# A four-layer hybrid decoder step: at three layer ends GpSimd adds the squares of the residual, and TensorE sums them with one product

## The reference

```python
def rms_norm(x, g):
    xf = x.astype(F32)
    y = xf * lax.rsqrt(jnp.mean(xf * xf, axis=-1, keepdims=True) + EPS)
    return (y * g.astype(F32)).astype(x.dtype)
...
for layer in range(DEPTH):
    h = rms_norm(x, g[0])
    y, ... = mixer(h, ...)
    x = x + rms_norm(y, g[1])
    h = rms_norm(x, g[2])
    y = memory_cross_attn(h, mem_k[layer], mem_v[layer], ...)
    x = x + rms_norm(y, g[3])
```

## Time and profile before

| | us |
|---|---|
| median of 3 runs | 2000.47 (1999.58 to 2001.61) |
| the profiled execution: its time | 2002.32 |
| the profiled execution: span from first to last instruction | 2000.5 |

### The profile page before, as it was taken

One profiled execution on the slowest core, in us unless ns is written; L12 is line 12 of the kernel. 1 busy time (PEld: TensorE's weight loads), 2 busy tenths in 40 slices (PEclk: granted clock), 3 DMA queues, 4 the chain that ended last, 5 costly groups with the idle time before them and its releaser, 6 DMA issues.

```text
span 2000.5 us, 35695 instructions
## 1 busy us (share of the span) xinstructions
PE 1946.4 (97%) x13930; PEld 1763.9 (88%) x13930; DVE 1243.0 (62%) x2220; ACT 929.5 (46%) x1555; POOL 1011.8 (51%) x1251
## 2 busy tenths in 40 slices
PE   9999999999999999999999999999999999999997
PEld 7998988798888998797889999998997889999976
DVE  6887434346887778655147877777464157874452
ACT  4767422344655555342354444443243347774333
POOL 5767623126555655150356666665641347776602
PEclk9999999999999999999999999999999999999998
DMA  5444567435444444486353444444586344455860
GB/s 172 141 137 143 160 220 261 167 100 175 130 131 133 139 135 153 124 298 235 116 169 109 131 131 131 144 144 149 161 306 221 130 146 137 139 158 167 286 231 27
DMA packets 332615, 324.64 MB, mean 162 GB/s; under 512 B 19768, under 2 KB 313056, under 8 KB 332448
## 3 DMA queue, kind: packets, MB, share of 16 engines
q1 hardware_dynamic: 330944, 321.49, 50.4%
q10 hardware_dynamic: 1504, 0.87, 0.2%
HBM read 292.16 MB, written 29.61 MB: 161 GB/s over the span
## 4 chain that ended last, share of the span: by engine, by line
PE 61%; DVE 9%; ACT 3%; issue 1%; DMA 1%; POOL 1%; SPq 0%; ACTq 0%; DVEq 0%
PE ps L773 8%; PE ps L774 8%; PE ps L778 8%; PE ps L1460 4%; PE ps L1263 3%; PE ps L1469 2%; PE ps L1526 2%; PE ps L763 2%; DVE work L2550 2%; PE ps L764 2%; PE ps L765 2%; PE ps L890 1%; PE ps L1337 1%; PE ps L1604 1%; PE ps L1543 1%
## 5 line engine op out<-in xcount | busy, mean ns | idle before, releaser
L1695 POOL TENSOR_TENSOR wl<-raw,wh 128x256 fp32r<-128x256 f32 x1216 | 1004.3, 861 | 956.6 <-ACT wh L1720 956.3
L1720 ACT ACTIVATE wh<-raw 128x1024 fp32r<-128x1024 f32 x302 | 309.8, 1053 | 207.9 <-PE ps L778 51.6
L773 PE MATMUL ps<-Hh,wh 128*128 128x320 f32 x1200 | 369.3, 321 | 2.5 <-DVE gate_area L2570 0.9
L774 PE MATMUL ps<-Hl,wh 128*128 128x320 f32 x1200 | 357.3, 311 | 0.0
L773 PEld LDWEIGHTS ps<-Hh,wh 128*128 128x128 f32 x1200 | 227.8, 190 | 10.3 <-DVE gate_area L2570 1.7
L774 PEld LDWEIGHTS ps<-Hl,wh 128*128 128x128 f32 x1200 | 227.9, 190 | 2.2
L2265 DVE TENSOR_SCALAR work<-ps 128x512 f32<-128x512 f32 (+8 forms) x220 | 100.4, 474 | 169.3 <-PE ps L873 39.8
L778 PE MATMUL ps<-Hh,wl 128*128 128x320 f32 x1200 | 200.7, 309 | 0.0
L778 PEld LDWEIGHTS ps<-Hh,wl 128*128 128x128 f32 x1200 | 182.6, 188 | 0.1
L773 PE MATMUL ps<-Oh,wh 128*128 128x320 f32 x512 | 152.2, 310 | 3.7 <-DVE Ol L3011 3.7
L774 PE MATMUL ps<-Ol,wh 128*128 128x320 f32 x512 | 151.1, 308 | 0.0
(11 more groups left out here) (442 smaller groups left out, 3923.6 us busy)
## 6 DMA issues: line engine op xcount, KB each, us to landing
raw<-rg_w_in SPq DMA_DIRECT2D x128, 256.0 KB, 3.6
raw<-hg_w_in SPq DMA_DIRECT2D x128, 256.0 KB, 5.0
raw<-ssd_w_in SPq DMA_DIRECT2D x96, 256.0 KB, 4.1
work<-cache_mem_k SPq DMA_DIRECT2D x40, 512.0 KB, 6.7
work<-cache_mem_v SPq DMA_DIRECT2D x40, 512.0 KB, 5.2
raw<-rg_w_out SPq DMA_DIRECT2D x64, 256.0 KB, 3.6
raw<-x_w_k SPq DMA_DIRECT2D x64, 256.0 KB, 3.6
raw<-x_w_v SPq DMA_DIRECT2D x64, 256.0 KB, 3.8
```

What stands on the lines that cost most here:

```text
L773: pe.matmul(ps[:, bank, 0:n], high(half, k), mh[:, k, 0:n], start=(k == 0), stop=False)
L774: pe.matmul(ps[:, bank, 0:n], high(half, k), ml[:, k, 0:n], start=False, stop=False)
L1695: ins = pool.tensor_tensor(out, src, wh[:, parted(n) % HALVES, r:r + 2].bitcast(F32), ALU.subtract)
L1720: act.activation(wh[:, nx.n % HALVES], raw[:, slot, :, half * P:(half + 1) * P], ACT.Copy).then_inc(hi_ready, 1)
```

## The change

`SQ[:, 0]` becomes the sum of all eight tiles by seven additions on POOL, each of which waits for its square and for POOL's own addition before. POOL counts `sq_pooled` after the last one. PE waits for that count and makes one product with ones where it made eight. `sq_pooled` is counted on the semaphore `consts`, behind the two counts that this has from the start of the kernel, so the instruction lists show a wait for `consts`.

```diff
+        shared = {"sq_pooled": ("consts", 1, 2), "lam_abs": ("par_read", 1, 2), ...
...
+        POOLED = KD - 1
...
+            def sum_pooled(L, n, bank):
+
+                pe.wait_ge(*past("sq_pooled", L + 1))
+                pe.matmul(ps[:, bank, 0:NT], ones[:], SQ[:, 0], start=True, stop=True).then_inc(S("ssq_full"), 1)
...
                 values(5, 0)
                 values(5, 1)
-                sum_squares(5 + 4 * L, 7)
+                sum_pooled(L, 5 + 4 * L, 7)
                 pe.wait_ge(*past("at_v_ready", XH * (L + 1) + 2))
                 values(4, 0)
                 values(4, 1)
...
+            def add_squares(L):
+                n = 5 + 4 * L
+                for k in range(1, POOLED + 1):
+                    pool.wait_ge(*past("sq_ready", n * KD + k + 1))
+                    if k > 1:
+                        steps.sync()
+                    ins = pool.tensor_tensor(SQ[:, 0], SQ[:, 0], SQ[:, k], ALU.add)
+                    if k < POOLED:
+                        steps.did(ins)
+                    else:
+                        ins.then_inc(S("sq_pooled"), 1)
+
             for n in PARTED:
+                if n in MIX_AT[1:]:
+                    add_squares(MIX_AT.index(n) - 1)
                 low(n)
```

More of the change, by code:

```diff
@@ L133, in trunk @@
         sems = {}
-        shared = {"lam_abs": ("par_read", 1, 2), "lb_diff": ("par_read", 1, 3), "sd_sel": ("par_read", 1, 4),
+        shared = {"sq_pooled": ("consts", 1, 2), "lam_abs": ("par_read", 1, 2), "lb_diff": ("par_read", 1, 3), "sd_sel": ("par_read", 1, 4),
                   "sd_dt_abs": ("par_read", 1, 5), "sd_dta": ("par_read", 1, 6),
```

## The result

The changed kernel is slower: 2006.3 us in the median of 7 runs, against 2000.59 us of 7 runs of the kernel before, a ratio of 1.0031 with a 95% interval of 1.0019 to 1.0042. I had forecast 1999.9 us and no measurable change, with a range to 2005.5. Measured three times more, each time beside the kernel before, it gave 1.0025 (1.0012 to 1.0038), 1.0028 (1.0017 to 1.0040) and 1.0023 (1.0014 to 1.0032). The loss is small, some 3 to 6 us, but it is there every time.

The account below looks back on a forecast made before the run. PE, busy 97% of the span, pays the eight products in full; removing 14 instructions an end, less POOL's late sum and half clock, wins 0.2 us, three ends 0.6: 2000.47 - 0.6 = 1999.9 us, range 1992.5 to 2005.5.

Parts of the forecast that it names:

- The port: Layer ends: DVE's residual and POOL's additions take turns on SBUF, 1.51 us a tile; PE waits 2.8 us for the sum.
- The addition: POOL at layer ends: additions of 128x320 spaced 0.84 us, some 0.95 us each with a hand-over as they depend on each other.
- The logarithm: ACT at a layer end: its logarithm begins at 1622.3 against 1623.10, 0.8 us won.
- The clock at the ends: Behind PE's 2.8 us wait: half clock at most of the three ends, leaving 0 to 0.3 us won, 0.2 taken.
- three ends 0.6: Whole kernel: 0.2 us won at each layer end, 0.6 for three, taken off the median of 2000.47 us.
- SP issues nothing new: SP at the layer ends: no new issues, and weight slots come free no later than the sum allows.
- The port held for whole instructions: Rival, DVE's residual beside the additions: 0.87 us held by each addition, 0.46 by each DVE instruction; 2006.2 us, chance 0.11.
- A longer low stretch: Rival, clock behind the wait: a longer half-clock stretch loses 3.0 us in `values`, ending 1.4 late; 2004.7 us, chance 0.05.
- E: Theory of the experiments, not of the prediction: the half clock behind the waits at the layer ends makes the loss.
- A: Theory of the experiments: ends cost nothing; later stages answer to the small time shift, by half-clock stretches and waits.

Follow-up runs that it names:

- filled: Changed kernel with five unused products on PE ahead of its wait at all three ends: 2001.94 us, 1.0001 to the kernel before; again 2000.73 us, 0.9996.
- with three tiles added: Changed kernel with POOL adding only tiles 1 to 3 into tile 0, PE summing the rest with five products: 1999.88 us, 0.9991 to the kernel before.
- with one product: Kernel before with only tile 7's product at the three ends, no additions, other squares left out of the sum: 1996.91 us, 0.9980.

## Why the prediction was wrong, step by step

- **The port.** Right, nearly to the digit. Forecast: pairs in turn, 1.51 us for a tile, the sum 2.8 us behind PE. Measured: 3.0 us for two tiles, 2.73 and 2.74. DVE's instruction beside an addition starts 1.07 to 1.08 us ahead of the next, the 1.08 worked out from the earlier trace rows.
- **The addition.** 857 to 1009 ns (median 927) for what I put at 0.84 and a hand-over; the hand-over is 0.14, so a second addition starts 1.15 us behind the first, while DVE keeps its 1.08. Without effect on the sum.
- **The logarithm.** Forecast 0.8 us earlier; counted from the start of the last product ahead of the sum it is 0.75 to 0.77 us earlier at eight of the 12 ends, and 0.1 to 0.6 at the other four, where the half clock already lies on the sum's own product.
- **The clock at the ends.** Forecast the low level at most of the ends: 8 of 12. Forecast 0 to 0.3 us won with it, I took 0.2: measured from the start of the last product, ends 0 and 1 lose 0.05 and end 2 wins 0.15 where it came, and an end where the clock held wins 0.75. The three ends together win 0.9 us in the mean of four traces, for the 0.6 of the forecast. That this is so near is partly luck: the ends at half clock win less than 0.2, and the four ends where the clock held make up for it.
- **The step that failed is "three ends 0.6"**: the sum was made at the three ends and handed on to the whole kernel unchanged, with nothing put down for the stages behind. In place of a gain of 0.6 us the kernel lost 3 to 6, with the ends themselves 0.9 us shorter. Nor does a gain arrive whole: 4.6 of 11.3 us, 2.7 and 3.2 of 6.45. What takes the rest is not shown in full. That a stage which begins earlier waits longer for other engines would be a plain reason, but the traces don't bear it out: PE's waits for POOL's `low` in the HGRN stage are 2.7 and 0.2 us in the two traces of before, 3.0 and 1.5 filled, 4.8 with three tiles added, 1.2 with one product. And the change moved something that I had not looked at, the place of the instruction fetches among the DMAs 400 us later. I wrote that SP issues nothing new; that is so, but a transfer that SP waits for became slower in all four traces.
- **The rivals.** The port held for whole instructions had 2006.2, the time that came. That is chance, for its mechanism did not come: it wanted the sum 1.1 us later than the eight products had it, and the sum was earlier at all 12 ends, by 0.1 to 0.8 us. A longer low stretch did not occur either. The loss had no rival of mine.

So the cause stays open in this: how much of the loss hangs on the half clock and how much on the fetches, since the fillers change both; a kernel with the waits filled and as many instructions of PE as the changed one would part them. Of the theories, E is left and, in another form than was tried, A: the later stages answer to where PE's instruction fetches fall. Open too is where the change at layer 1's end alone loses (its trace does not show the long wait at the seventh write, and its profiled execution took 2001.2 us, the shortest of 12 with a median of 2006.17), why that at layer 0's end alone loses, and the last 0.8 to 1.7 us.

## What to carry to other kernels

A gain or a loss read at one place is not the kernel's: ask what the next stages are waiting for, and count on a part of the gain only. Where PE has to wait for a sum, give the other engine only as much of it as is done when PE arrives, and let PE do the rest: here four of seven additions. And where 5 us of 2000 are at stake, compare several traces of each kernel before a stage is blamed; what stands in all four of one and in none of 16 others is worth a look, and still no proof.

## What the runs showed of the hardware that I had not expected

- Where a fetch of instructions began during a write of 128 KB, the write landed later: 4.6 instead of 3.3 us from the write's issue to the load that waits for it (medians of 65 and 75 cases; five of the 65 were not late). Adding or removing instructions on PE moves these meetings about.
- The half clock behind a wait of 2.7 to 2.8 us came at 13 of 18 ends that had such a wait, in nine traces, and at none of the nine filled ends. The same wait in the same program can be followed by it or not.
